# A gated linear recurrence on one core: its two directions run side by side instead of one after the other

## The chip, the cores and the metric

The kernel runs on one core of one Trainium2 chip. Its time is the device time of one execution in microseconds (us). Three executions of the kernel before took 5386.82, 5388.15 and 5391.06 us; the median is 5388.15. The engines of the core work side by side and wait for each other by semaphores: TensorE (PE in the profile; PEld is its loading of weights), VectorE (DVE), ScalarE (ACT), GpSimd (POOL) and SyncE (SP, which here only issues DMAs).

## The reference, cut to what matters

The program is a whole model: two hybrid layers (convolution, attention, Fourier mixing and a gated recurrence) and a second block. The change touches the recurrence alone, which each of the two hybrid layers holds once, in two directions over the positions:

```python
S_t = diag(f_t) S_{t-1} + k_t v_t^T          # per head, 64 x 64, four heads
o_t = S_t^T q_t
# in chunks, a = cumsum(log f) inside the chunk:
inter  = (q * exp(a)) @ state                # what earlier chunks give
scores[t, s] = sum_k q[t,k] k[s,k] exp(a[t,k] - a[s,k])   for s <= t
intra  = scores @ v
s_new  = exp(a_last) * state + (k * exp(a_last - a))^T @ v
```

Direction 0 goes from the first position to the last, direction 1 from the last to the first; both results are added. There are 10 tiles of 128 positions, two of them context. Layer 0 wants outputs for all 10; layer 1 wants them for 8 and runs the two context tiles only for the state. The kernel takes a chunk to be 128 positions.

## The kernel before

`recurrence` works on one direction. `mixer_layer` calls it twice, one block of the program after the other, with a barrier of all engines between them. Inside, one step of the loop is one tile of 128 positions (variable `u`). The scores of a tile can't be one product, since exp(a[t] - a[s]) may not be split into two factors at will. They are split into seven **levels**, `LEVELS = [64, 32, 16, 8, 4, 2, 1]`: at the level of half-width h the queries in one half of each 2h-wide group meet the keys in the other half, both scaled by exponentials relative to the boundary between the halves. An eighth product (`NL`) gives the diagonal. For each level:

- POOL subtracts the boundary value from the sums `a` (two instructions of 128x128 for each level, 14 for a tile) into `X`. There are two `X` buffers, taken in turn by tile.
- ACT exponentiates a whole `X` (one instruction of 1792 columns), and also gives `eq` and `ke`.
- DVE multiplies both halves by queries and keys (`scale_level`, two instructions for each level, 14 for a tile; `scale` for `ke` and `qe`).
- PE multiplies: four heads, each 128x128 with a contraction over 64 rows. The profile shows each float32 matmul as two records, so that two levels (one group g, of which a tile has four) are 16 records. A group goes to one of two pairs of PSUM banks, taken in turn.
- DVE copies all 128 columns of all four heads from PSUM to `sc`, only where the level's mask is set (`copy_predicated`, L1175, eight for a tile). Each such copy waits for the one before it, since all write `sc`.

When all eight copies are done PE makes the outputs of the tile (L1263 and L1264, 16 records), DVE copies them to `o` (L1197) or adds them (L1199, direction 1), and only then copies the first group of the next tile. Beside this, PE turns `ke` (L1219), ACT copies it from PSUM to `ket` (L1112), PE makes the state products (L1253), and DVE updates the state `S` (L1187).

In layer 0, PE also makes one piece of the modulation matrix for each tile (`Modulations.products`, L2565 and L2568, 72 records): its weights are a 2 MB chunk loaded by SP into a ring of three slots, and ACT evacuates it.

The order on each engine is the order in which the code is written; no scheduler moves anything.

Of the kernel before, what the change touches and what calls it, by code (L numbers as in the profile page):

```python
# [12 lines left out]
P = 128  # L13
# [1010 lines left out]
def recurrence(k, direction, q, key, a, v, o, outputs, lay, mods=None, moves=()):  # L1024

# [4 lines left out]
    X = [lay(f"x{i}", [P, NL, 2, P]) for i in range(2)]  # L1033
    eq = [lay(f"eq{i}", [P, 2, P]) for i in range(2)]
    qe = [lay(f"qe{i}", [P, 2, P]) for i in range(2)]
    ke = lay("ke", [P, 2, P])
    ket = lay("ket", [P, BR])
    sc = lay("sc", [P, 2, 2, P])
    masks = lay("masks", [P, NL + 1, P])
    S = [lay(f"s{i}", [P, 2, HD]) for i in range(2)]  # L1040
    order = [0, 1] + list(range(CT_, NT)) if direction == 0 else [1, 0] + list(range(NT - 1, CT_ - 1, -1))
    edge = P - 1 if direction == 0 else 0
    query_half = 1 if direction == 0 else 0
    want = [t in outputs for t in order]
    n_out = np.concatenate([[0], np.cumsum(want)]).astype(int).tolist()
    (masks_in, x_exped, subbed, exped, chain, scaled, products, masked, ke_t, ket_out, s_ready, state_out,
     o_ready, o_out, moved) = sems = k.sems(
        "masks_in", "x_exped", "subtracted", "exped", "dve_chain", "scaled", "level_products", "masked",
        "ke_transposed", "ket_out", "state_products", "state_out", "o_ready", "o_out", "moved")


    PAIRS = (NL + 1) // 2

    def halves(view, h):

        r = view.rearrange("p c (n s h) -> p c n s h", s=2, h=h)
        return [r[:, :, :, i, :] for i in range(2)]

    with nc.Block() as block:
        @block.sync  # L1060
        def _(sp):
            sp.dma_start(masks[:, :, :], d["level_masks"][direction]).then_inc(masks_in, 16)
            for dst, src in moves:
                sp.dma_start(dst, src).then_inc(moved, 16)
            k.ws.load_until(sp, k.ws.taken)
            if moves:
                sp.wait_ge(moved, 16 * len(moves))

        @block.gpsimd
        def _(pool):  # L1070
            for u, t in enumerate(order):
                if not want[u]:
                    continue
                j = n_out[u]
                at = a[:, :, t * P:(t + 1) * P]
                if j >= 2:
                    pool.wait_ge(products, PAIRS * (j - 1))
                for l, h in enumerate(LEVELS):
                    xa, xb = halves(X[j % 2][:, l, :, :], h)
                    aa, ab = halves(at, h)  # L1080
                    b = aa[:, :, :, h - 1:h] if direction == 0 else ab[:, :, :, 0:1]
                    b = b.to_broadcast([P, 2, P // (2 * h), h])
                    pool.tensor_tensor(xa, *((b, aa) if query_half else (aa, b)), ALU.subtract)
                    ins = pool.tensor_tensor(xb, *((ab, b) if query_half else (b, ab)), ALU.subtract)
                ins.then_inc(subbed, 1)

        @block.scalar
        def _(act):
            if mods:
                mods.load_bias(act, mods.first)  # L1090
                mods.load_bias(act, mods.first + 1)
            for u, t in enumerate(order):
                at = a[:, :, t * P:(t + 1) * P]
                if u >= 2:
                    act.wait_ge(state_out, u - 1)
                act.activation(eq[u % 2][:, :, :], at, ACT.Exp)
                if u >= 1:
# [2260 lines left out]
```

## Time and profile before

| what | value |
|---|---|
| median of three runs | 5388.15 us |
| the profiled execution | 5394.52 us, span 5392.5 us |
| recurrence, layer 0, both directions | 917.9 to 1259.5 us of the span |
| recurrence, layer 1, both directions | 2214.9 to 2500.3 us |
| busy over the whole span | PE 81%, DVE 53%, ACT 34%, POOL 11% |

The page of the profile gives these shares as a mean over stages with different limits. The change lies in two stretches that together are 627 us long, some 12% of the span. How long one tile takes there, and what ends each wait, is read from two views. The windows give one row for each stretch: its bounds and length in us, then the busy us and number of instructions of PE, PEld, DVE, ACT and POOL, the clock granted to TensorE as a share of 2.4 GHz (so 0.50 is 1.2 GHz and 1.00 is 2.4 GHz), the DMA share and GB/s. The timeline gives one row for each instruction, or run of equal ones: start in us, length in us, engine, line, operation, output<-inputs, shapes, count, and in brackets the idle time of the engine before it and what ended it. Starts of neighbouring rows give the pitch, which is less than the length where instructions overlap in an engine's pipeline.

### The profile page before, as it was taken

Reading aid. Unit: us, or ns where it says so; the run is one execution under the profiler, and the core shown is the slowest. Engines: PE = TensorE matmul, PEld = TensorE weight load, DVE = VectorE, ACT = ScalarE, POOL = GpSimd, SP = SyncE. Lnnn points to the kernel's source line nnn. Section 1 sums busy time; section 2 is a strip of 40 time slices with the busy share of each in tenths; the row PEclk is TensorE's granted clock in tenths of the full one; section 3 lists DMA queues with packets and bytes.
Section 4 is the critical chain, followed back from the end, with each engine's and each line's share of the span. In section 5 each row is a group of like instructions: output and inputs, shape, how many; then the busy total and the mean of one; then the engine's idle time right before and its main releaser. Section 6 shows DMA issues by size and latency. Waiting matters only on the chain. (4 is left out here: it accounts for less than half of the span.)

```text
span 5392.5 us, 56133 instructions
## 1 busy us (share of the span) xinstructions
PE 4351.5 (81%) x21480; PEld 3266.6 (61%) x21480; DVE 2869.4 (53%) x4265; ACT 1822.4 (34%) x3173; POOL 616.7 (11%) x858
## 2 busy tenths in 40 slices
PE   5758887877875988666677999997764969899898
PEld 4644576766664566555554655556652657688777
DVE  3454347665545546666543454542556745566545
ACT  3322245222432226312431333333322444344333
POOL 0001000330000100231001211110004500011100
PEclk7867899767887999767888999998886979899999
DMA  4000012333400011101200000003000054211134
GB/s 149 24 16 0 20 41 84 136 130 114 136 24 19 0 37 40 55 5 48 99 16 16 8 4 4 4 1 122 19 1 2 1 184 160 55 47 47 55 129 144
DMA packets 173564, 296.36 MB, mean 55 GB/s; under 512 B 43434, under 2 KB 94634, under 8 KB 173300
## 3 DMA queue, kind: packets, MB, share of 16 engines
q1 hardware_dynamic: 172548, 292.56, 16.1%
q8 instruction: 173, 2.83, 0.2%
q0 software_dynamic: 608, 0.08, 0.1%
q14 instruction: 91, 0.75, 0.0%
q10 hardware_dynamic: 144, 0.15, 0.0%
HBM read 262.25 MB, written 30.51 MB: 54 GB/s over the span
## 5 line engine op out<-in xcount | busy, mean ns | idle before, releaser
L319 DVE TENSOR_TENSOR x_low<-buf_a,x_high 128x1280 fp32r<-128x1280 f32 (+4 forms) x336 | 336.8, 1002 | 603.8 <-ACT x_high L297 602.0
L344 PE MATMUL ps<-x_high,w_high 128*128 128x256 f32 (+1 forms) x1344 | 492.4, 366 | 91.8 <-DVE w_low L323 89.1
L957 ACT ACTIVATE pt<-ps 128x512 f32<-128x512 f32 (+1 forms) x488 | 289.7, 594 | 752.3 <-PE ps L900 750.8
L297 ACT CAST x_high<-buf_a 128x1280 fp32r<-128x1280 f32 (+4 forms) x336 | 292.9, 872 | 726.6 <-PE ps L346 596.2
L910 PE MATMUL ps<-pt,v 128*128 128x512 f32 (+1 forms) x976 | 508.3, 603 | 0.0
L345 PE MATMUL ps<-x_low,w_high 128*128 128x256 f32 (+1 forms) x1344 | 486.8, 362 | 0.0
L346 PE MATMUL ps<-x_high,w_low 128*128 128x256 f32 (+1 forms) x1344 | 483.8, 360 | 0.0
L981 DVE TENSOR_REDUCE mx<-ps 128x1 f32<-128x1280 f32 (+1 forms) x200 | 289.8, 1449 | 350.9 <-PE ps L867 349.4
L2955 PE MATMUL ps<-w_high,x_high 128*128 128x512 f32 x896 | 369.6, 413 | 105.5 <-DVE w_low L2828 60.4
L2956 PE MATMUL ps<-w_low,x_high 128*128 128x512 f32 x896 | 362.8, 405 | 0.0
L2957 PE MATMUL ps<-w_high,x_low 128*128 128x512 f32 x896 | 362.7, 405 | 0.0
L344 PEld LDWEIGHTS ps<-x_high,w_high 128*128 128x128 f32 x1344 | 260.7, 194 | 153.7 <-DVE x_low L319 107.6
L2828 DVE TENSOR_TENSOR w_low<-w,w_high 128x1024 fp32r<-128x1024 f32 x170 | 208.2, 1225 | 255.6 <-ACT w_high L2925 255.6
L344 PE MATMUL ps<-w_high,x_high 128*128 128x512 f32 (+2 forms) x608 | 217.5, 358 | 110.6 <-DVE w_low L323 107.0
L898 PE MATMUL ps<-q_high,k_high 97*128 97x512 f32 (+3 forms) x488 | 292.1, 599 | 11.1 <-DVE q_low L994 11.1
L1003 DVE RECIPROCAL rec<-ps 64x512 f32<-64x512 f32 (+1 forms) x52 | 168.0, 3231 | 249.6 <-PE ps L910 249.6
L2925 ACT CAST w_high<-w 128x1024 fp32r<-128x1024 f32 x170 | 178.2, 1048 | 337.8 <-PE ps L2957 337.7
L2259 PE MATMUL ps<-x_high,w_high 128*128 128x512 f32 x704 | 278.2, 395 | 12.4 <-DVE w_low L2355 12.4
L346 PEld LDWEIGHTS ps<-x_high,w_low 128*128 128x128 f32 x1344 | 259.5, 193 | 39.0
L345 PEld LDWEIGHTS ps<-x_low,w_high 128*128 128x128 f32 x1344 | 260.7, 194 | 33.8
L2261 PE MATMUL ps<-x_high,w_low 128*128 128x512 f32 x704 | 279.6, 397 | 0.0
L2260 PE MATMUL ps<-x_low,w_high 128*128 128x512 f32 x704 | 278.9, 396 | 0.0
(388 smaller groups left out, 8757.9 us busy)
## 6 DMA issues: line engine op xcount, KB each, us to landing
w<-in_w_out SPq DMA_DIRECT2D x26, 2048.0 KB, 8.0
w<-in_w_mod SPq DMA_DIRECT2D x24, 2048.0 KB, 8.1
w<-in_w_down SPq DMA_DIRECT2D x15, 2048.0 KB, 7.9
w<-in_w_in SPq DMA_DIRECT2D x14, 2048.0 KB, 8.5
w<-in_w_up SPq DMA_DIRECT2D x22, 1024.0 KB, 7.6
w<-in_w_in SPq DMA_DIRECT2D x12, 1024.0 KB, 5.1
x<-in_x SPq DMA_DIRECT2D x16, 512.0 KB, 3.9
scratch_x<-x SPq DMA_DIRECT2D x16, 512.0 KB, 5.2
```

Source lines behind the costliest of these rows:

```text
L297: act.copy(xh[i % NX][:, 0:s["tn"]], x_of(s)).then_inc(x_high, 1)
L319: dve.tensor_tensor(xl[i % NX][:, 0:s["tn"]], x_of(s), xh[i % NX][:, 0:s["tn"]].bitcast(F32), ALU.subtract).then_inc(x_low, 1)
L344: pe.matmul(g["out"], lhs[0][:, :], rhs[0][:, :], start=(s["kk"] == 0), stop=False)
L345: pe.matmul(g["out"], lhs[0][:, :], rhs[1][:, :], start=False, stop=False)
L346: mm = pe.matmul(g["out"], lhs[1][:, :], rhs[0][:, :], start=False, stop=s["last"])
L898: pe.matmul(o, hi, qh[u % 2][r0:r1, 0:nq], start=True, stop=False)
L910: pe.matmul(ps[:, 6 + u % 2, 0:w["nq"]], w["v"](i), pt[g % NPT][:, 0:w["nq"]], start=(i == 0), stop=(i == n - 1)).then_inc(pv_done, 1)
L957: act.activation(pt[g % NPT][:, 0:w["nq"]], ps[:, 4 + g % 2, 0:w["nq"]], ACT.Exp, scale=scale).then_inc(exped, 1)
L981: dve.tensor_reduce(mx[u % 2][:, i:i + 1], src, AX.X, ALU.max).then_inc(maxed, 1)
L2955: pe.matmul(o, a[:, t], wh[i % NW][:, c], start=(s["kk"] == 0), stop=False)
L2956: pe.matmul(o, a[:, t], wl[i % NW][:, c], start=False, stop=False)
L2957: mm = pe.matmul(o, b[:, t], wh[i % NW][:, c], start=False, stop=s["last"])
```

## The change

One call of `recurrence` now runs both directions. A class `Scan` holds a direction's buffers, semaphores and its order of tiles, and the list `D2` holds the two. Every engine goes through the tile step by group, and inside a group does direction 0 and then direction 1:

- Each direction has one `x` buffer (not two), its own pair of PSUM banks for the level products (banks 0 and 1, or 2 and 3; a group has to be copied out before the next of that direction is made), and its own bank for keys and state (4 or 5). The output banks 6 and 7 are shared by the two in turn.
- POOL, ACT and the scaling on DVE work group by group for the next tile, each as soon as the group of this tile has been multiplied.
- A level's copy covers only the columns that are queries at that level (64 of 128 in each head, read and written with gaps for the small levels). The diagonal's copy stays whole.
- The outputs of tile u-1 are made at the start of tile u.
- The modulation pieces go two for each step of both directions, in free columns of banks 4 and 5, behind groups 2 and 3.
- The reload of `YT[:, 0:4]` from memory (2.5 MB), which ran beside direction 0, is now issued in `recurrence_norm`, whose SP waits for it at its end.
- `o` is written by whichever direction comes to a tile first, and the other adds.

The core of the diff (`r` is a `Scan`, G is 4):

```diff
+            for g in range(G):
+                for r in D2:
+                    subtract(r, first, g)
+            for u in range(first, NU - 1):
+                for g in range(G):
+                    for r in D2:
+                        pool.wait_ge(r.products, G * n_out[u] + g + 1)
+                        subtract(r, u + 1, g)
...
-                        dve.copy_predicated(
-                            sc[:, :, :, :].rearrange("p a b c -> p (a b) c"),
-                            masks[:, l, :].bitcast(U32).unsqueeze(1).to_broadcast([P, 4, P]),
...
+                    if l < NL:
+                        h = LEVELS[l]
+                        to, heads = (x.rearrange("p g (n s h) -> p g n s h", s=2, h=h)[:, :, :, r.query_half, :]
+                                     for x in (to, heads))
...
+                for g in range(G):
+                    for r in D2:
+                        if g == 0 and n_out[u]:
+                            output(r, u - 1)
+                        copies(r, u, g)
+                        if g == 0:
+                            scale_levels(r, u, G - 1)
+                        elif u + 1 < NU:
+                            scale_levels(r, u + 1, g - 1)
+                        if g == 1:
+                            state(r, u)
+                        if g == 2 and u + 1 < NU:
+                            scale(r, u + 1)
...
+            def level_products(r, u, g):
+                j = n_out[u]
+                pe.wait_ge(r.x_scaled, G * j + g + 1)
+                if j or g:
+                    pe.wait_ge(r.masked, (NL + 1) * j + 2 * g)
...
+                for g in range(G):
+                    for r in D2:
+                        if g == 0 and n_out[u]:
+                            outputs_of(r, u - 1)
+                        level_products(r, u, g)
+                        if g == 0:
+                            turn_keys(r, u)
+                        if g == 1:
+                            states(r, u)
+                    if mods and g >= 2:
+                        pe.wait_ge(D2[g - 2].state_out, u + 1)
+                        mods.products(pe, mods.first + 2 * u + g - 2)
...
-    for direction in range(2):
-        lay = Layout(k, A_A, A_B)
...
+    recurrence(k, q, key, a, v, o, range(nt0, NT), Layout(k, A_A, A_B), mods)
+    recurrence_norm(k, layer, o, YT, nt0, Layout(k, A_A, A_B), [(YT[:, 0:4, :], done_rows)])
```

How this moves instructions on VectorE, in the middle of a tile of layer 0. Before: `sc` is the score buffer, `x_152` one of the two operand buffers; a copy (L1175) stands between the two multiplications (L1154) of each level, and after the last of them the state (L1187) and the output.

```order
L1154 TENSOR_TENSOR x_152_6739<-x_152_6739,q_5132 128x4x32
L1175 COPY_PREDICATED sc_6747<-masks_6748,ps 128x512
L1154 TENSOR_TENSOR x_152_6739<-x_152_6739,key_125_5130 128x8x16
L1154 TENSOR_TENSOR x_152_6739<-x_152_6739,q_5132 128x8x16
L1175 COPY_PREDICATED sc_6747<-masks_6748,ps 128x512
L1154 TENSOR_TENSOR x_152_6739<-x_152_6739,key_125_5130 128x16x8
L1154 TENSOR_TENSOR x_152_6739<-x_152_6739,q_5132 128x16x8
L1175 COPY_PREDICATED sc_6747<-masks_6748,ps 128x512
L1154 TENSOR_TENSOR x_152_6739<-x_152_6739,key_125_5130 128x32x4
L1154 TENSOR_TENSOR x_152_6739<-x_152_6739,q_5132 128x32x4
L1175 COPY_PREDICATED sc_6747<-masks_6748,ps 128x512
L1154 TENSOR_TENSOR x_152_6739<-x_152_6739,key_125_5130 128x64x2
```
After: `sc_159` and `x_152` belong to direction 0, `sc_171` and `x_164` to direction 1; the shapes of the copies (L1159) show the gaps.

```order
L1159 COPY_PREDICATED sc_159_6746<-masks_160_6747,ps 128x16x16
L1159 COPY_PREDICATED sc_159_6746<-masks_160_6747,ps 128x32x8
L1138 TENSOR_TENSOR x_152_6739<-x_152_6739,key_125_5130 128x2x64
L1138 TENSOR_TENSOR x_152_6739<-x_152_6739,q_5132 128x2x64
L1138 TENSOR_TENSOR x_152_6739<-x_152_6739,key_125_5130 128x4x32
L1138 TENSOR_TENSOR x_152_6739<-x_152_6739,q_5132 128x4x32
L1164 SCALAR_TENSOR_TENSOR s_161_6748<-s_162_6749,eq_154_6741,ps 128x64 x2
L1159 COPY_PREDICATED sc_171_6757<-masks_172_6758,ps 128x16x16
L1159 COPY_PREDICATED sc_171_6757<-masks_172_6758,ps 128x32x8
L1138 TENSOR_TENSOR x_164_6750<-x_164_6750,q_5132 128x2x64
L1138 TENSOR_TENSOR x_164_6750<-x_164_6750,key_126_5131 128x2x64
L1138 TENSOR_TENSOR x_164_6750<-x_164_6750,q_5132 128x4x32
```
The copies now come in pairs of one direction, of 256 columns instead of 512, and the multiplications of that direction for the next tile (L1138) follow each pair.

How it moves them on TensorE, around the start of a tile. Before: the first group of a tile (`x_153`, L1243 x8), the keys' turn (L1219), two groups at once, the modulation piece (L2565, L2568), the last group, the state products (L1253) and the outputs (L1263, L1264) of the same tile.

```order
L1243 MATMUL ps<-x_153_6740 128x128 x8
L1219 MATMUL ps<-ident_49,ke_6745 128x128 x2
L1243 MATMUL ps<-x_153_6740 128x128 x16
L2565 MATMUL ps<-w_2_50,act_c_55 2x128 x32
L2568 MATMUL ps<-bias_148_6736,one_56 2x128 x4
L1243 MATMUL ps<-x_153_6740 128x128 x4
L1243 MATMUL ps<-q_5132,key_125_5130 128x128 x4
L1253 MATMUL ps<-v_5133,ket_6746 64x64 x4
L1263 MATMUL ps<-v_5133,sc_6747 128x64
L1264 MATMUL ps<-s_163_6750,qe_157_6744 128x64
L1263 MATMUL ps<-v_5133,sc_6747 128x64
L1264 MATMUL ps<-s_163_6750,qe_157_6744 128x64
```
After: the outputs of direction 1 for the tile before (`sc_171`, L1263 and L1264), then one group (L1249 x8) of each direction in turn, with the keys' turn (L1223) and the state products (L1231) between them.

```order
L1264 MATMUL ps<-s_173_6759,qe_167_6753 128x64
L1263 MATMUL ps<-v_5133,sc_171_6757 128x64
L1264 MATMUL ps<-s_173_6759,qe_167_6753 128x64
L1249 MATMUL ps<-x_164_6750 128x128 x8
L1223 MATMUL ps<-ident_49,ke_169_6755 128x128 x2
L1249 MATMUL ps<-x_152_6739 128x128 x8
L1231 MATMUL ps<-v_5133,ket_158_6745 64x64 x4
L1249 MATMUL ps<-x_164_6750 128x128 x8
L1231 MATMUL ps<-v_5133,ket_170_6756 64x64 x4
L1249 MATMUL ps<-x_152_6739 128x128 x8
L1249 MATMUL ps<-x_164_6750 128x128 x8
L2586 MATMUL ps<-w_3_51,act_c_55 2x128 x32
```
The outputs have gone from the end of their tile to the first group of the next, and no two groups of one direction stand next to each other.

## Rows read from the trace of the kernel before

**Rows 1.** Windows: the four direction blocks; busy us of each engine, TensorE clock, DMA.

```profile
917.00:1089.00 172.00, 136.94 (x1620) 115.01 (x1620) 106.95 (x272) 40.50 (x92) 56.09 (x141) 0.71 0.44 154
1089.00:1259.00 170.00, 136.75 (x1620) 114.63 (x1620) 107.33 (x272) 39.08 (x90) 56.37 (x140) 0.70 0.37 128
2214.00:2359.50 145.50, 95.70 (x740) 80.48 (x740) 88.76 (x224) 26.78 (x49) 43.84 (x112) 0.69 0.10 37
2359.50:2500.00 140.50, 95.82 (x740) 80.41 (x740) 87.24 (x224) 25.48 (x48) 44.32 (x112) 0.68 0.02 5
```
**Rows 2.** Timeline of VectorE, one tile (start, us, ..., idle before).

```profile
949.41 1.56 DVE L1175 COPY_PREDICATED sc<-masks,ps 128x512 f32<-128x512 uint32 x2 [1.49 <-PE ps L1243]
...
953.03 0.28 DVE L1154 TENSOR_TENSOR x<-x,q 128x128 f32<-128x128 f32 x1
953.23 0.75 DVE L1175 COPY_PREDICATED sc<-masks,ps 128x512 f32<-128x512 uint32 x1
953.87 0.28 DVE L1154 TENSOR_TENSOR x<-x,key 128x128 f32<-128x128 f32 x1
...
957.47 0.49 DVE L1154 TENSOR_TENSOR x<-x,q 128x128 f32<-128x128 f32 x1
957.88 0.72 DVE L1175 COPY_PREDICATED sc<-masks,ps 128x512 f32<-128x512 uint32 x1
...
959.99 0.46 DVE L1187 SCALAR_TENSOR_TENSOR s<-s,eq,ps 128x64 f32<-128x64 f32 x2
963.77 0.42 DVE L1197 COPY o<-ps 128x256 f32<-128x256 f32 x1 [3.32 <-PE ps L1264]
965.68 0.73 DVE L1175 COPY_PREDICATED sc<-masks,ps 128x512 f32<-128x512 uint32 x1 [1.49 <-PE ps L1243]
```
**Rows 3.** Timeline of TensorE, the same tile and the outputs before it.

```profile
943.18 0.43 PE L1263 MATMUL ps<-v,sc 128*128 128x64 f32 x2 [1.72 <-DVE sc L1175]
943.54 0.43 PE L1264 MATMUL ps<-s,qe 64*128 64x64 f32 x2
...
949.21 0.69 PE L1219 MATMUL ps<-ident,ke 128*128 128x128 f32 x2
949.82 2.60 PE L1243 MATMUL ps<-x 64*128 64x128 f32 x32
952.35 1.93 PE L2565 MATMUL ps<-w,act_c 128*2 128x128 f32 x64
...
955.63 0.45 PE L1253 MATMUL ps<-v,ket 128*64 128x64 f32 x8
958.75 0.66 PE L1263 MATMUL ps<-v,sc 128*128 128x64 f32 x2 [2.67 <-DVE sc L1175]
959.34 0.69 PE L1264 MATMUL ps<-s,qe 64*128 64x64 f32 x2
...
963.42 2.12 PE L1243 MATMUL ps<-x 64*128 64x128 f32 x15
```
**Rows 4.** Windows: TensorE's granted clock in three short stretches.

```profile
951.00:953.00 2.00, 2.00 (x50) 1.86 (x50) 1.60 (x4) 1.79 (x2) 0.00 (x0) 1.00 0.00 0
959.00:961.00 2.00, 2.00 (x8) 1.65 (x8) 1.45 (x5) 0.00 (x0) 2.00 (x6) 0.50 1.05 404
2640.00:2660.00 20.00, 10.55 (x48) 8.25 (x46) 13.17 (x23) 9.42 (x21) 0.00 (x0) 0.91 0.33 105
```
**Rows 5.** Timeline of VectorE: first copies of both layers, one scaling.

```profile
933.82 1.57 DVE L1175 COPY_PREDICATED sc<-masks,ps 128x512 f32<-128x512 uint32 x2 [2.18 <-PE ps L1243]
...
2234.75 0.28 DVE L1154 TENSOR_TENSOR x<-x,q 128x128 f32<-128x128 f32 x1
...
2237.28 1.58 DVE L1175 COPY_PREDICATED sc<-masks,ps 128x512 f32<-128x512 uint32 x2 [1.87 <-PE ps L1243]
```
**Rows 6.** DMA issues, start of layer 0's first block: KB each, us to landing.

```profile
buf_b<-scratch_branches SPq DMA_DIRECT2D x1, 2560.0 KB, 13.8
```
**Rows 7.** Timeline of SyncE: first DMA of the stage after `recurrence_norm`, layer 0.

```profile
1280.29 0.81 SPq L2970 DMA_DIRECT2D gate_row<-scratch_mod  x2
```

More of the change, by code:

```diff
@@ L1021, with recurrence @@
 NL = len(LEVELS)
-def recurrence(k, direction, q, key, a, v, o, outputs, lay, mods=None, moves=()):
+def recurrence(k, q, key, a, v, o, outputs, lay, mods=None):
     nc, ps, d = k.nc, k.ps, k.d
[L1033 to L1044, printed above, removed]
-    n_out = np.concatenate([[0], np.cumsum(want)]).astype(int).tolist()
[L1046 to L1057, printed above, removed]
+    D2 = [Scan(k, i, q, key[i], a[i], outputs, lay) for i in range(2)]
+    NU = NT
+    want = [t in outputs for t in D2[0].order]
+    n_out = np.concatenate([[0], np.cumsum(want)]).astype(int).tolist()
+    first = want.index(True)
+    G = (NL + 1) // 2
+    levels_of = lambda g: [l for l in (2 * g, 2 * g + 1) if l < NL]
+    writer = {}
+    for u in range(NU):
+        for r in D2:
+            if want[u]:
+                writer.setdefault(r.order[u], (r, n_out[u] + 1))
     with nc.Block() as block:
@@ L1202, in _, with scale @@
[L1202 to L1206 removed]
+            def scale(r, u):
+                dve.wait_ge(r.exped, u + 1)
+                dve.tensor_tensor(r.ke[:, :, :], r.ke[:, :, :], r.tile(r.key, u), ALU.mult).then_inc(r.ke_scaled, 1)
+                if want[u]:
+                    dve.tensor_tensor(r.qe[n_out[u] % 2][:, :, :], r.eq[u % 2][:, :, :], r.tile(r.q, u),
+                                      ALU.mult).then_inc(r.qe_scaled, 1)
@@ new lines, in turn_keys, with states @@
+            def turn_keys(r, u):
+                pe.wait_ge(r.ke_scaled, u + 1)
+                if u >= 1:
+                    pe.wait_ge(r.state_out, u)
+                    if mods:
+                        pe.wait_ge(mods.evacuated, 2 * (u - 1) + r.direction + 1)
+                for c in range(2):
+                    mm = pe.transpose(ps[:, r.keys_bank, c * P:(c + 1) * P], r.ke[:, c, :], k.ident[:, :])
+                mm.then_inc(r.ke_t, 1)
+            def states(r, u):
+                pe.wait_ge(r.ket_out, u + 1)
+                t = r.order[u]
@@ L1266, in recurrence @@
-    k.done(sems + (mods.sems if mods else []))
-def recurrence_norm(k, layer, o, yt, t_from, lay):
+                mm.then_inc(r.s_ready, 1)
+            def level_products(r, u, g):
+                j = n_out[u]
+                pe.wait_ge(r.x_scaled, G * j + g + 1)
+                if j or g:
+                    pe.wait_ge(r.masked, (NL + 1) * j + 2 * g)
+                for half in range(2):
+                    l = 2 * g + half
+                    for h in range(4):
+                        c, par = divmod(h, 2)
+                        p0 = par * HD
+                        x = y = r.x[p0:p0 + HD, min(l, NL - 1), c, :]
+                        if l == NL:
+                            x, y = r.tile(r.key, u)[p0:p0 + HD, c, :], r.tile(r.q, u)[p0:p0 + HD, c, :]
+                        o0 = c * 256 + half * P
+                        mm = pe.matmul(ps[:, r.bank + par, o0:o0 + P], x, y, start=True, stop=True)
+                mm.then_inc(r.products, 1)
@@ L1271, in recurrence_norm @@
+            for r in D2:
+                outputs_of(r, NU - 1)
+    k.done(D2[0].sems + D2[1].sems + (mods.sems if mods else []))
+def recurrence_norm(k, layer, o, yt, t_from, lay, moves):
     nc, ps, d = k.nc, k.ps, k.d
```

351 lines of the change are left out of this document (173 added, 178 removed).

## The prediction

> **What bounds the kernel now.** I looked first at the busy shares of the page, which name no single bound, and then at the windows over the two stretches that the change touches. The four direction blocks are 172, 170, 145.5 and 140.5 us long [rows 1], 628 us together, about 627 without the barriers at the edges. In none is an engine full: in a layer 0 block VectorE is busy 107 of 172 us, POOL 56, ACT 40. TensorE shows 137, but at a mean clock of 0.71, so much of that is work at half speed. What bounds a block is a chain, and the timeline of VectorE shows it. A tile is one lap: the first copy at 949.41, the same copy of the next tile at 965.68, so 16.3 us. VectorE is occupied from 949.4 to 960.5, then stands 3.32 us until the outputs are made, copies them for 0.42 us and stands again for 1.49 us until the first level group of the next tile is there [rows 2]. TensorE meanwhile stands 2.67 us before those outputs, and when it starts they run at a pitch of 0.59 to 0.62 us for two records, against 0.36 us in the tile before (943.18 to 943.54), and the first group after them takes 2.12 us for 15 records, against 2.60 us for 32 in the middle of the tile [rows 3]. The granted clock is 0.50 in the first place and 1.00 in the second [rows 4]. So each engine waits for the other once a tile, and TensorE's wait also costs it half its clock in the part that VectorE waits for.
>
> Steady laps give 15.5 us on average in layer 0: from the first copy at 933.8 to the end of that block at 1088 are 154 us for ten tiles, the start being 16 us [rows 1, 5]. In layer 1 the first copy is at 2237.3, 22.4 us after the start, and eight tiles take the remaining 122 us, 15.3 us each. A pair of tiles, one of each direction, costs 31.0 and 30.6 us. Below, P0 and P1 are what such a pair costs after the change.
>
> **VectorE's work for a pair.** The whole copy lasts 0.73 to 0.75 us, the next instruction starts 0.64 us after it (953.23 to 953.87), and two linked by their wait take 1.56 us, so a link costs about 0.8 us in all [rows 2]. Nothing here copies half the columns. The nearest rows are the instructions without a mask: 128 columns last 0.28, 256 last 0.42 us [rows 2], 0.14 us for each 128. Off 0.73 that makes 0.45 us for 256 columns, which I take; the other end is 0.73, if gaps cost as much as they save. A linked pair of half copies is then 0.45 + 0.08 + 0.37 = 0.9 us, and the last group, with the whole diagonal, 0.45 + 0.08 + 0.64 = 1.17. For each direction: three pairs 2.7, last 1.17, 14 multiplications at 0.20 (953.03 to 953.23) 2.8, ke and qe 0.7, state 0.46 + 0.08, outputs 0.42, in sum 8.3 us. A pair takes 16.7 us, against about 22 now (11.1 a tile, without the waits).
>
> The gaps are the point where a rule speaks against the change. The last multiplication of a tile, whose operands in SBUF alternate element by element, lasts 0.28 us like the one of the widest level [rows 2, 5], so gaps in SBUF are free here; gaps read from PSUM no row shows. The Trainium skill ("SBUF — State Buffer", section "Door 1: The DMA port swizzle") says that SBUF has lines of 16 bytes and PSUM of 8, that an access to a new line pays a penalty, and that gaps in PSUM slow matmuls significantly. For SBUF the trace doesn't agree; for PSUM it is silent, and I keep the case below as a rival, with its price from rows.
>
> POOL's subtractions now lie beside VectorE's work, no longer mostly in its idle time. Where both run, a multiplication starts 0.41 instead of 0.20 us after the last (957.47 to 957.88) while a copy stays at 0.72 [rows 2]. POOL is busy 5.6 us a tile [rows 1], 11.2 us a pair, near half of the time, so half of 32 such instructions pay 0.21 us: 3.3 us; the ends are 0 and 6.7. VectorE's sum is 16.7 + 3.3 = 20.
>
> **TensorE's work for a pair.** At full clock: eight groups of 16 records at 0.08 us (2.60 us for 32) are 10.2 us; outputs 2 x 16 x 0.18 (0.36 for two) 5.8; keys' turn 2 x 0.3, half of the 0.61 between 949.21 and 949.82; state products 2 x 0.45; modulation, layer 0 only, 2 x 2.2 (1.93 and the bias rows behind it) 4.4 [rows 3]. Together 21.9 in layer 0, 17.5 in layer 1. At half clock: groups 2 x 8 x 1.1 = 17.5, outputs 9.9 (0.62 for two), the rest doubled, 39 and 30.4 us. I expect full clock nearly throughout: waits in the new order are under 1.5 us, and TensorE holds 0.91 in a stretch where it is busy 10.6 of 20 us [rows 4]; but 959.3 shows what one wait of 2.67 us does.
>
> **The laps.** Go through the four groups g, with both directions in each. At g = 0 TensorE has 2 x (2.9 + 1.28 + 0.3) = 9.0 us and VectorE 3.4; at g = 1 TensorE 3.5 and VectorE 4.5; at g = 2 they have 2.6 (4.8 with the modulation) and 4.9; at g = 3 2.6 (4.8) and 3.9. A group of a direction may follow only when its previous one is copied, and VectorE does that while TensorE makes the other direction's group. In layer 0 VectorE falls behind by about 1 us at g = 1 and g = 2 and catches up during g = 3 and the outputs; the lap is TensorE's 21.9 us. In layer 1 VectorE leads from g = 1 to g = 3: 9.0 + 4.5 + 4.9 + 3.9 = 22.3, less some 1.4 us by which the last copies run beside the next outputs, 20.9. To both I add 2.5 us, that part of POOL's 3.3 us that falls outside g = 0, and wake-ups. P0 = 24.5, P1 = 23.5.
>
> The wait between the two outputs (the shared banks 6 and 7: direction 1 must wait for direction 0's copy, 0.42 us) is hidden, since a group and a turn of keys, 1.6 us, stand between them on TensorE. POOL (11.2) and ACT (40.5 / 10, so 8 a pair and some 1.5 for three more starts of each exponential [rows 1]) have half of the lap free; each step of theirs is for the next tile. Two 2 MB weight chunks in 24.5 us replace one in 15.5; each has two laps of slack in a ring of three.
>
> **What is saved once.** A second block's start goes in each layer, and the start that stays has both directions in it: twice the subtractions, but no 2.5 MB reload beside the masks. I leave it as it is, 16 and 22 us [rows 1, 5]. The end costs what the last lap saves by having no next tile. The reload took 13.8 us to land [rows 6]; `recurrence_norm` lasts from 1259 to 1280 [rows 1, 7], so it stays hidden, as it would in layer 1, whose stage is some 3 us shorter. If that cover failed it would cost at most a few us.
>
> **The sum.** Layer 0: 16 + 10 x 24.5 = 261. Layer 1: 22 + 8 x 23.5 = 210. Together 471 for 627, a gain of 156 us. Off the profiled execution's own 5394.5 that is 5238.5; that execution lies 6.4 us over the median, so off the median 5388.15 it is **5232 us**. In the general form the two stretches take 38 + 10 P0 + 8 P1, and no gain is left at 10 P0 + 8 P1 = 589.
>
> **The rivals.**
> - *TensorE alone is the bound.* POOL's share hurts only where VectorE has slack. P0 = 22, P1 = 21: 426, gain 201, 5187 us. For it: half of VectorE's collisions fall at g = 0. Against it: every hand-over of a single bank pair costs a wake-up.
> - *Copies with gaps are no cheaper.* The half copy stays at 0.73, 14 x 0.28 = 3.9 us a pair. Layer 0 hides most of it: P0 = 26, P1 = 27.2, together 516, gain 111, 5277 us. By the rule of the Trainium skill on PSUM lines (same page and section) this, or more, would be the cost of the copies of the small levels.
> - *The clock keeps falling.* TensorE, fed in bursts of 1.3 us, is at half speed half of the time: P0 = (21.9 + 39) / 2 = 30.5, P1 26.5, together 555, gain 72, 5316 us. For it: 0.68 to 0.71 over the blocks now [rows 1]. Against it: its long waits are what goes.
> - *The slower side: half clock throughout.* The alternation leaves TensorE waiting at each group, so that it never gets its clock back; then P0 = 39 and P1 = 30.5, together 672, 45 us more, 5433 us. It decides when over about two thirds of TensorE's work in layer 0 is at 1.2 GHz. Against it: at half clock in layer 0 TensorE would have no wait at all, and a run without waits got its clock back here, by 951 [rows 4].
>
> **How the numbers follow.** My forecast has 52%, TensorE alone 15%, no cheaper copies 14%, the falling clock 14%, the slower side 3%, and 2% for no difference through something I haven't seen. About 0.2% (11 us) is what a measurement can tell from no change. The range, 5175 to 5325, takes in the three milder rivals with the ends of the half copy and of POOL's share, and leaves out the slower side. Faster 0.95, within 0.2% 0.02, slower 0.03.
>
> **What would show it.** In the profile after: one block for each layer, near 261 and 210 us; the same copy of one direction every 24 us; half copies at 0.45 us; TensorE's clock over 0.9 in the block, and outputs at 0.36 us for two records; VectorE's longest waits at g = 0, for the outputs' end. Half copies near 0.73, a block clock under 0.8, or multiplications at 0.41 nearly everywhere would prove a step wrong, and with P0 over 28 the forecast is.

## The result, and the profile after

The changed kernel takes 5267.52 us (median of 4 runs, 5256.10 to 5277.01); before, on the same chip, 5389.60 (5386.82 to 5398.37). The ratio is 0.9766 with a 95% interval of 0.9753 to 0.978, so 2.3% faster. The forecast was 5232 us with a range of 5175 to 5325: the side and the range hold, the median is 35.5 us over the forecast. The profiled execution took 5277.01 us.

The page after, busy time by engine over the whole span:

```profile
PE 4310.9 (82%) x21480; PEld 3235.0 (61%) x21480; DVE 2825.0 (54%) x4265; ACT 1845.9 (35%) x3281; POOL 612.5 (12%) x858
```

As before, that doesn't show the change. The windows do. Each hybrid layer now has one recurrence block, here from its first DMA (the masks) to the first DMA of `recurrence_norm` (columns as in [rows 1]); the last two rows are 25 us out of the middle of each:

```profile
918.12:1168.36 250.24, 216.05 (x3240) 180.71 (x3240) 189.70 (x544) 91.99 (x241) 109.75 (x280) 0.90 0.51 183
2128.93:2375.67 246.74, 197.43 (x1480) 166.37 (x1480) 156.87 (x448) 63.35 (x145) 86.74 (x224) 0.63 0.04 14
...
1015.00:1040.00 25.00, 22.04 (x373) 18.65 (x377) 21.56 (x63) 10.30 (x26) 13.09 (x34) 1.00 0.48 170
...
2260.00:2285.00 25.00, 20.74 (x159) 17.48 (x158) 18.58 (x53) 7.14 (x16) 10.74 (x28) 0.64 0.01 1
```

Cut in the same way, the blocks before were 341.6 and 285.4 us. The sum goes from 627.0 to 497.0, 130 us less (forecast 156). The profiled executions differ by 117.5 us (5394.52 and 5277.01); the other 12.6 us are in stages that the change doesn't touch, 0.2 ahead of the first block, 5.1 between the two and 7.3 behind the second. Among all the traces of this study the stretch between the blocks is 955.4 to 961.7 us long, and the one ahead of the first block 903.9 to 919.6, though its code is the same in all; I take both for variation from run to run, and what sets them was not looked into. A difference of some 15 us between two single executions can therefore come from outside the blocks. The blocks vary too: four traces in which the layer 0 block is the same code show 247.2 to 254.9 us for it, and layer 1's unchanged block 244.8 to 246.7. Differences of some 8 us in layer 0 mean nothing below.

The two rows in the middle are the finding: in the middle of layer 0 TensorE is at its full clock (0.90 over the whole block), in layer 1 it has a granted clock of 0.64, less than in the old blocks (0.68 to 0.71, [rows 1]).

Timeline of TensorE after, one lap of layer 0 (the copy of direction 0's first group starts at 1004.64, and again at 1028.42):

```profile
1001.04 0.43 PE L1264 MATMUL ps<-s,qe 64*128 64x64 f32 x2
1001.40 0.43 PE L1263 MATMUL ps<-v,sc 128*128 128x64 f32 x2
...
1013.42 1.16 PE L1249 MATMUL ps<-x 64*128 64x128 f32 x16
1015.74 1.16 PE L1249 MATMUL ps<-x 64*128 64x128 f32 x16 [1.16 <-DVE sc L1159]
1016.83 1.93 PE L2586 MATMUL ps<-w,act_c 128*2 128x128 f32 x64
1018.69 0.40 PE L2589 MATMUL ps<-bias,one 1*2 1x128 f32 x8
...
1021.18 0.72 PE L1249 MATMUL ps<-x 64*128 64x128 f32 x8 [1.00 <-DVE sc L1159]
```

Two waits of about 1 us are left, and the outputs stand at a pitch of 0.36 us; in [rows 3] there was one wait of 2.67 us and outputs at 0.59. The same in layer 1:

```profile
2276.32 0.72 PE L1249 MATMUL ps<-x 64*128 64x128 f32 x8 [2.10 <-DVE sc L1159]
2276.84 0.64 PE L1249 MATMUL ps<-q,key 64*128 64x128 f32 x8
2278.98 1.23 PE L1249 MATMUL ps<-x 64*128 64x128 f32 x8 [1.50 <-DVE sc L1159]
2279.97 1.09 PE L1249 MATMUL ps<-q,key 64*128 64x128 f32 x8
2281.67 0.69 PE L1263 MATMUL ps<-v,sc 128*128 128x64 f32 x2 [0.61 <-DVE sc L1159]
2282.29 0.69 PE L1264 MATMUL ps<-s,qe 64*128 64x64 f32 x2
...
2286.37 2.12 PE L1249 MATMUL ps<-x 64*128 64x128 f32 x15
```

Three waits follow one another (2.10, 1.50, 0.61). The group at 2278.98 is already twice as long as the one at 2276.32, and outputs and first group run at half speed, at 0.62 and 2.12 us as in [rows 3]. The old fault is back in this layer.

Timeline of VectorE after: in layer 0 a pair of copies of the groups g = 1, 2 and 3; then, in layer 1, the lap's start, its longest wait and its end:

```profile
1014.69 0.90 DVE L1159 COPY_PREDICATED sc<-masks,ps 128x256 f32<-128x256 uint32 x2
...
1017.26 1.23 DVE L1159 COPY_PREDICATED sc<-masks,ps 128x256 f32<-128x256 uint32 x2
...
1024.59 1.48 DVE L1159 COPY_PREDICATED sc<-masks,ps 128x256 f32<-128x256 uint32 x2
```

```profile
2259.71 0.92 DVE L1159 COPY_PREDICATED sc<-masks,ps 128x256 f32<-128x256 uint32 x2 [1.39 <-PE ps L1249]
...
2264.96 0.42 DVE L1177 COPY o<-ps 128x256 f32<-128x256 f32 x1 [3.53 <-PE ps L1264]
...
2288.52 0.92 DVE L1159 COPY_PREDICATED sc<-masks,ps 128x256 f32<-128x256 uint32 x2 [1.39 <-PE ps L1249]
```

A pair of half copies takes 0.90 us as forecast for half-widths 64 to 8. The pair of 4 and 2 takes 1.2, that of 1 and the diagonal 1.5: single copies last 0.42 to 0.44 us down to half-width 4, and 0.73 to 0.75 at 2 and 1, as long as a whole one [rows 2]. The layer 1 lap is 2288.52 - 2259.71 = 28.81 us.

### The profile page after: what moved, and what is told of

It reads as the page before. It is cut to its first block and busy times, and to the rows that moved or that the text cites. A ratio compares the mean times of both kernels' runs of the same rounds, so it can differ in the third digit from the quotient of the medians.

```text
span 5275.2 us, 56171 instructions
## 1 busy us (share of the span) xinstructions
PE 4310.9 (82%) x21480; PEld 3235.0 (61%) x21480; DVE 2825.0 (54%) x4265; ACT 1845.9 (35%) x3281; POOL 612.5 (12%) x858
## 3 DMA queue, kind: packets, MB, share of 16 engines
q1 hardware_dynamic: 172548, 292.56, 16.3%
```

## The experiments

My theory after the result: in layer 1, which has no modulation work, TensorE's waits cost it its clock, and the half clock costs the missing 5 us a lap. The rivals: VectorE's dearer small copies, or POOL's share of its time. Each run is given as a ratio to the kernel before, timed on the same chip (medians there 5395.47, 5393.97 and 5397.81 us for the three sets), and with its two blocks (layer 0 / layer 1), cut as above; the changed kernel has 250.2 / 246.7.

**filled.** Unneeded matmuls behind groups 2 and 3 of layer 1, into a free part of a bank, all on the same two rows.

```diff
+            def fill(n):
+                for i in range(n):
+                    pe.matmul(ps[0:2, 6, 256:384], k.ident[:, 0:2], k.ident[:, :], start=True, stop=True,
+                              skip_group_check=True)
...
+                        if not mods:
+                            fill({(2, 0): 16, (2, 1): 24, (3, 0): 20, (3, 1): 8}.get((g, r.direction), 0))
```

> The changed kernel, with unneeded small matmuls (2 output rows, never read) in layer 1 alone, where TensorE waits for the copies: 16 behind direction 0's group 2, 24 behind direction 1's, 20 and 8 behind the two of group 3; at the 0.029 us a record seen for the modulation matmuls that is some 4 us of added TensorE work for each pair of tiles. Theory (the clock in layer 1 falls because TensorE waits 1.5 to 2.1 us at groups 2 and 3, and the outputs that follow then run at half speed): the granted clock in layer 1 rises from 0.64 to over 0.9, a pair of tiles falls from 28.8 to 22.5 to 24 us, the block from 247 to about 205, the time by about 40 us against the changed kernel. Rival (VectorE or the hand-over of the banks sets the lap in layer 1): the lap stays at 28 to 29 us or grows by the added work, up to 33 us.

Measured: 5291.44 us, 0.9804 [0.9787, 0.982], blocks 250.3 / 272.0: slower than without, where the theory had 40 us less. The timeline of TensorE says why:

```profile
2251.96 3.65 PE L1269 MATMUL ps<-ident 128*2 128x128 f32 x32
2255.55 1.16 PE L1249 MATMUL ps<-x 64*128 64x128 f32 x16
2256.64 5.40 PE L1269 MATMUL ps<-ident 128*2 128x128 f32 x48
...
2270.45 0.43 PE L1263 MATMUL ps<-v,sc 128*128 128x64 f32 x2
2270.81 0.43 PE L1264 MATMUL ps<-s,qe 64*128 64x64 f32 x2
...
2273.21 1.16 PE L1249 MATMUL ps<-x 64*128 64x128 f32 x15
```

The clock is back (outputs at 0.36, first group 1.16, granted clock 0.95 over the block), but a record of the filling took 0.114 us (3.65 / 32) where the modulation's takes 0.030 (1.93 / 64), so the filling itself became the bound. The modulation's matmuls go to four groups of rows in turn; these wrote the same rows every time.

**filled4.** The same numbers of matmuls, spread over four groups of rows.

```diff
+                    q = 32 * (i % 4)
+                    pe.matmul(ps[q:q + 2, 6, 256:384], k.ident[:, 0:2], k.ident[:, :], start=True, stop=True,
```

> As the run filled, but the unneeded matmuls of layer 1 write to four groups of output rows in turn (as the modulation matmuls do, 0.029 us a record), where those of the run filled all wrote to the same two rows and took 0.115 us a record. So 0.93, 1.4, 1.2 and 0.5 us of added TensorE work at the four places, not 3.7, 5.4, 4.5 and 1.9. Theory (the clock in layer 1 falls through TensorE's waits, and full clock is worth 5 us a lap): clock in the block over 0.9, lap 22.5 to 24.5, block 200 to 215 us, 30 to 45 us under the changed kernel. Rival (what the clock gives back, the added matmuls and VectorE's chain take): lap 27 to 29, the same time within 8 us.

Measured: 5251.14 us (5245.18 to 5254.91), 0.973 [0.9712, 0.9748], blocks 254.9 / 236.0. It is the fastest version that leaves nothing out: all its runs are under all of **after_again**, the changed kernel once more on the same chip.

> The changed kernel itself, beside the others on the same chip: 5260 to 5275 us, laps of 23.8 and 28.8 us, as a base for the differences.

That gave 5268.70 us (5257.05 to 5277.63), 0.9762 [0.974, 0.9784], blocks 247.2 / 246.6. Its median is 17.6 us over that of filled4. The two profiled executions differ by 13.1 us, of which layer 1 gives 10.6, the unchanged stretch ahead of the first block another 10.6, and layer 0 takes 7.7 back. The gain falls short of the 30 to 45 us of the theory, and the expected lap of 22.5 to 24.5 us was missed; it is 27.2 (the filling's records now take 0.031 to 0.033 us). The timeline of TensorE in filled4:

```profile
2203.00 1.49 PE L1270 MATMUL ps<-ident 128*2 128x128 f32 x48
...
2207.23 0.71 PE L1249 MATMUL ps<-x 64*128 64x128 f32 x8 [0.45 <-DVE sc L1159]
...
2209.93 0.43 PE L1263 MATMUL ps<-v,sc 128*128 128x64 f32 x2 [0.99 <-DVE sc L1159]
...
2212.11 0.46 PE L1263 MATMUL ps<-v,sc 128*128 128x64 f32 x2
...
2212.89 2.12 PE L1249 MATMUL ps<-x 64*128 64x128 f32 x15
```

Two short waits stay, and the clock falls in the middle of the outputs; the first group is at half clock again. The block's clock is 0.74. So the clock is worth at least the 10.6 us by which this block is shorter than in after_again. The slow filling of `filled`, which left no wait at all, held the clock; a quick one that leaves none was not tried. Why layer 1 loses its clock at waits (0.45 and 0.99) that layer 0 stands (1.16 and 1.00) is open.

**fewer_products.** Layer 0 with less work for TensorE: one of eight row blocks of each modulation piece.

```diff
-        for kk in range(KD):
+        for kk in range(KD if self.first == 0 else 1):
```

> The changed kernel with one of the eight row blocks of the modulation products left out of all that are made beside the recurrence of layer 0 but the first (8 of the 64 records of a piece stay, with the bias), so about 1.6 us less TensorE work for each piece, 3.2 us for a pair of tiles. Theory (layer 0 has its full clock only because the modulation pieces fill TensorE's waits): layer 0's clock falls from 0.93 to 1.00 to about 0.65, its lap grows from 23.8 to 27 to 29 us though it has less to do, and the time grows by 30 to 50 us. Rival (TensorE's work sets the lap, the clock is independent of it): the lap falls by up to 3 us, to 21 us, and the time by up to 30 us.

Measured: 5307.43 us, 0.9838 [0.9824, 0.9853], blocks 298.1 / 244.8. TensorE has 3.1 us less to do in each lap, two pieces of 1.93 us shrunk to 0.40, and layer 0 is 48 us slower (the median of the whole kernel 40 us, 30 to 50 were expected): its clock fell from 0.90 to 0.62. In the timeline of TensorE the pattern of layer 1 appears in layer 0:

```profile
1047.72 1.23 PE L1249 MATMUL ps<-x 64*128 64x128 f32 x8 [1.04 <-DVE sc L1159]
...
1053.38 0.69 PE L1263 MATMUL ps<-v,sc 128*128 128x64 f32 x2
1053.99 0.69 PE L1264 MATMUL ps<-s,qe 64*128 64x64 f32 x2
```

This is the strongest evidence for the theory: nothing but TensorE's own work was changed, and downward.

**full_copies.** Only the copies are widened again to all 128 columns.

```diff
-                    if l < NL:
+                    if l < 0:
```

> The changed kernel with all copies over all 512 columns again: this undoes the copies over query columns alone. By the durations in the trace after (0.44 us for half-widths 64 to 4, 0.73 for 2 and 1, whole 0.74) each pair of tiles gets 2 x 5 x 0.30 = 3.0 us more on VectorE. Theory (VectorE leads only in groups 1 to 3): layer 0's lap grows by 1 to 2.5 us, layer 1's by 2 to 3 us, together 25 to 50 us more than the changed kernel. Rival (the narrow copies gave nothing, the order of the work gave all): the same time within 10 us.

Measured: 5295.23 us, 0.9816 [0.9798, 0.9834], blocks 277.2 / 251.1. The narrow copies are worth 27 us in layer 0, part of it by the clock (0.82 instead of 0.90), and 4 in layer 1, where VectorE has waits of 3.5 us to fill. The median is 28 us over that of the changed kernel, inside the 25 to 50 expected, but layer 1's lap grew by 0.6 us and not by 2 to 3.

**less_pool.** Three of seven levels of POOL's subtractions for later tiles are gone (POOL is busy 69 instead of 110 us in layer 0). The exponentials are taken of zero times the input, so the scores are not the reference's.

```diff
-                for l in levels_of(g):
+                for l in levels_of(g) if u == first else levels_of(g)[-1:]:
...
-                act.activation(x, x, ACT.Exp).then_inc(r.x_exped, 1)
+                act.activation(x, x, ACT.Exp, scale=0.0).then_inc(r.x_exped, 1)
```

> The changed kernel with POOL doing only the last level's two subtractions of each group for all tiles but the first, and the level exponentials taken of zero times the input (so the scores are not the reference's, the instructions of all other engines and their shapes are the same). POOL's instructions for a pair of tiles fall from 28 to 16. Theory (POOL costs VectorE about 0.2 us for each multiplication that meets it, worth 2.5 us of the lap in my sum): layer 0's lap falls by 1 to 1.5 us and layer 1's by as much, 15 to 25 us in all. Rival (these collisions fall where VectorE waits for TensorE anyway): laps within 0.5 us, under 10 us in all.

Measured: 5247.94 us, 0.9724 [0.971, 0.9739], blocks 246.5 / 236.5. The median is 19.6 us under that of the changed kernel, inside the 15 to 25 expected, and 14 us of it are in the blocks of the traces; the laps of layer 0 gained 0.4 us where 1 to 1.5 were expected, those of layer 1 gained 1.3. A multiplication lasts 0.30 us on average, not 0.36. So POOL's share of VectorE's time is worth 10 us in layer 1, and in layer 0 no more than that block varies, for three sevenths of its instructions: real, but not the missing 37, and the clock in layer 1 stayed at 0.63.

**before_narrow.** The other way round: the old order, with the narrow copies alone.

```diff
+                        if l < NL:
+                            h = LEVELS[l]
+                            to, heads = (x.rearrange("p g (n s h) -> p g n s h", s=2, h=h)[:, :, :, query_half, :]
+                                         for x in (to, heads))
```

> The kernel before with one part of the change alone: copies over query columns only, for all seven levels (the level products lie in PSUM as in the changed kernel so that four heads' halves can be read). By the durations in the trace after, five of the eight copies of a tile get 0.30 us shorter, 1.5 us for each tile. Theory (the lap of one direction is a chain through VectorE, so nearly all of it counts): 36 tiles by 1.0 to 1.5 us, 36 to 54 us off, so 5335 to 5355. Rival (TensorE waits less for the outputs but makes them at the same half clock, and its own groups become the bound): 5 to 30 us off.

Measured: 5377.31 us (10 runs), 0.9967 [0.9955, 0.9978], blocks 335.6 / 269.6. Only 17 us (of 5393.97; by the two blocks of the traces 22); the theory's 36 to 54 are missed. Timeline of VectorE there:

```profile
950.61 0.42 DVE L1136 TENSOR_TENSOR ke<-ke,key 128x256 f32<-128x256 f32 x1 [0.83 <-ACT ke L1100]
...
952.20 0.29 DVE L1154 TENSOR_TENSOR x<-x,key 128x128 f32<-128x128 f32 x1 [0.48 <-ACT x L1106]
...
962.32 0.42 DVE L1203 COPY o<-ps 128x256 f32<-128x256 f32 x1 [3.35 <-PE ps L1270]
```

Much of the time taken off the copies turned up as waits for ACT. In the same tile of the kernel before they are only 0.26 us for `ke` and 0.17 for `x`; over all tiles they grew from 17.0 to 35.6 us and from 6.5 to 18.4. The wait for the outputs at half clock stayed as it was (3.32 before).

**whole_small.** In the changed kernel the copies at half-widths 2 and 1 are whole again.

```diff
-                    if l < NL:
+                    if l < 5:
```

> The changed kernel with the two copies of half-widths 2 and 1 whole again, the other five narrow. In the trace after, these last 0.73 to 0.75 us for 256 columns, as much as 0.74 for 512. Theory (runs of one or two 4-byte elements cost twice, so narrowing them saves nothing): the same time as the changed kernel within 6 us, copies of 0.73. Rival (the whole copies are slower where POOL or TensorE also reads, or the pair's link differs): 10 us more.

Measured: 5264.66 us (5258.28 to 5271.19), 0.9761 [0.9743, 0.9779], blocks 249.7 / 244.6: the same as the changed kernel. Narrowing these two gains nothing.

**dense_a and dense_b.** Which operand's gaps cost? For half-width 2, a makes the PSUM source dense and b the mask; for 1, a makes destination and mask dense and b the destination alone. A dense operand takes the first 64 columns of each head, so wrong columns are copied.

```diff
+                        dense = {2: ('heads',), 1: ('to', 'which')}.get(h, ())      # dense_a
+                        dense = {2: ('which',), 1: ('to',)}.get(h, ())              # dense_b
```

> The changed kernel, with the operands' gaps taken away in part (wrong columns, so the scores are not the reference's): for half-width 2 the PSUM source is read densely and destination and mask keep their gaps; for half-width 1 destination and mask are dense and the PSUM source keeps its gaps. If the gaps in PSUM are what costs, half-width 2 falls from 0.73 to 0.44 us and half-width 1 stays at 0.74; if it is the gaps in SBUF (destination or mask), half-width 2 stays and half-width 1 falls to 0.44.

> As the run dense_a, with other operands: for half-width 2 the mask alone is dense, for half-width 1 the destination alone. If the mask's gaps cost, half-width 2 falls to 0.44 us; if the destination's, half-width 1 falls; if the PSUM source's, both stay at 0.73.

Measured: 5260.80 and 5267.22 us in a single run each, blocks 247.8 / 242.5 and 247.8 / 242.7. Timeline of VectorE in dense_a, the pair of half-widths 4 and 2, and then the pair of 1 and the diagonal:

```profile
2269.73 1.18 DVE L1162 COPY_PREDICATED sc<-masks,ps 128x256 f32<-128x256 uint32 x2
...
2272.59 1.19 DVE L1162 COPY_PREDICATED sc<-masks,ps 128x256 f32<-128x256 uint32 x2
```

The same two pairs in dense_b:

```profile
2273.01 1.17 DVE L1162 COPY_PREDICATED sc<-masks,ps 128x256 f32<-128x256 uint32 x2
...
2275.87 1.19 DVE L1162 COPY_PREDICATED sc<-masks,ps 128x256 f32<-128x256 uint32 x2
```

With source or mask dense, the pair of 4 and 2 stays at 1.2. With the destination dense, the pair of 1 and the diagonal falls from 1.5 to 1.19, in both kernels, with the PSUM source still read at every second element. The destination's gaps cost; those of source and mask are free in these copies. The copy at half-width 4, in runs of four float32, pays nothing; runs of two and of one pay the same.

**before_filled and before_filled_narrow.** How much of the gain is the clock alone? The old order, with 44 unneeded matmuls (28 in the second) for each wanted tile, ahead of the outputs.

```diff
+                    for i in range(44):
+                        r0 = 32 * (i % 4)
+                        pe.matmul(ps[r0:r0 + 2, 6, 256:384], k.ident[:, 0:2], k.ident[:, :], start=True, stop=True,
+                                  skip_group_check=True)
```

> The kernel before, with 44 unneeded small matmuls (four groups of output rows in turn, never read) between the state products and the outputs of each wanted tile, about 2.5 us of TensorE work in a wait of 2.7 to 3.0 us. Nothing else of the change is in it. Theory (half clock is what makes the outputs and the next first group slow, so the interleaving gains in part by keeping the clock): outputs at 0.36 instead of 0.62 us for two records, first group 1.2 instead of 2.1 us, some 3 us for each of 36 tiles, 70 to 110 us off. Rival (the clock isn't tied to this wait, or the added work delays the outputs): within 15 us of the kernel before.

> The run before_filled with the narrow copies as well and 28 matmuls (1.6 us) for the shorter wait: both gains that need no second direction. Theory (clock and copies are two separate gains, and side by side adds the overlap of the two chains to them): 15 to 50 us under before_filled, and still above the changed kernel with its clock kept, since each tile keeps VectorE's wait of 2.5 to 3 us for outputs and first group. Rival (all that the change gave is clock and copies): as fast as the changed kernel or faster, 5220 to 5265.

Measured: 5327.98 us (5325.86 to 5328.95), 0.9873 [0.9853, 0.9893], blocks 302.9 / 251.8, and 5290.71 us (5289.38 to 5316.34), 0.9816 [0.9788, 0.9843], blocks 293.3 / 247.1. Timeline of TensorE in before_filled, one tile of layer 0:

```profile
968.55 2.58 PE L1261 MATMUL ps<-ident 128*2 128x128 f32 x88
971.24 0.44 PE L1267 MATMUL ps<-v,sc 128*128 128x64 f32 x2
971.60 0.43 PE L1268 MATMUL ps<-s,qe 64*128 64x64 f32 x2
...
974.00 1.16 PE L1243 MATMUL ps<-x 64*128 64x128 f32 x15
```

The wait of 2.67 us is filled; outputs at 0.36, first group at 1.16. Useless work in an idle stretch takes 70 us off a kernel in which nothing else is changed, the lower edge of what was expected; the granted clock of the blocks is 0.88 and 0.85 (0.70 and 0.68 before). On top of it the narrow copies bring 37 us by the medians, twice the 17 they bring without it. The profiled execution of before_filled_narrow is the slowest of its four (5316.34 us), and its blocks are only 14 us shorter than those of before_filled. Its tiles in layer 0 show what held it back. Two windows, each from the start of one filling to the start of the next:

```profile
954.15:969.44 15.29, 14.68 (x223) 12.41 (x219) 9.72 (x30) 3.88 (x9) 5.65 (x15) 0.78 0.40 140
969.44:981.11 11.67, 11.57 (x223) 9.66 (x219) 8.65 (x27) 3.88 (x9) 5.50 (x15) 1.00 0.50 183
```

Timeline of TensorE, the start of the outputs in the first of them:

```profile
956.48 0.43 PE L1273 MATMUL ps<-v,sc 128*128 128x64 f32 x2 [0.61 <-DVE sc L1185]
```

The first seven such stretches of the block alternate. In one the outputs follow the filling at once, the clock stays full, and it takes 11.7 us. In the other a wait of 0.61 us is left behind the filling, the clock falls in the middle of the outputs, and it takes 15.3. Two of the short kind, 23.3 us, are as short as the changed kernel's average lap in layer 0 (23.4, below). Each short one but the first follows a long one, in which ACT and POOL may get ahead, so a steady 11.7 is not shown; a filling that leaves no wait beside the narrow copies was not tried.

## Why the prediction was right, and where its sum was wrong

**The bound, read from [rows 2 to 4]: shown.** The prediction took the old block for a chain in which one wait of TensorE also costs half its clock. On one chip the steps are: before 5397.8, with the clock mostly held 5328.0, with narrow copies too 5290.7, side by side 5268.7. So 70 of the 129 us are to be had by the clock alone, 37 by the narrow copies once the clock is held better, and 22 are left. Each step is a difference of medians; for the last the intervals of the ratios (0.9788 to 0.9843, and 0.974 to 0.9784) just don't touch, and by the blocks of the profiled executions the last two steps are 14 and 47. How these 59 us divide is therefore uncertain, and that the last step is due to the new order as such is not shown: in the profiled execution the old order lost its clock in every second tile of a long row, and was as fast as the new one in the others. The order is not needed to hold the clock: filling the wait raised it to 0.88 and 0.85. In layer 0 it holds most of it without useless work (0.90), in layer 1 it doesn't (0.63).

**What is saved once: right.** The first copies start 16.3 us (934.46) and 21.4 us (2150.35) after the block, forecast 16 and 22. `recurrence_norm` with the reload takes 20.8 us in layer 0 as before, so the reload is hidden:

```profile
1168.36 0.37 SPq L1305 DMA_DIRECT2D gain<-in_hgrn_norm_g  x1
1168.78 0.46 SPq L1307 DMA_DIRECT2D buf_b<-scratch_branches  x1
1189.20 0.82 SPq L2991 DMA_DIRECT2D gate_row<-scratch_mod  x2
```

**P0 = 24.5: a little high, and close in part by luck.** Ten laps take 1168.36 - 934.46 = 233.9 us, 23.4 each. In the lap from 1004.64 to 1028.42 TensorE works 23.78 - 2.16 = 21.6 us, forecast 21.9, but two errors cancel there: a group of 16 records has a pitch of 1.09 us at full clock and not 1.3 (the 2.60 us for 32 records in [rows 3] began at half clock), and this lap runs some 1.6 us longer because its first groups are at half clock. In a lap all at full clock TensorE works 20.07 us and waits 2.2. Laps of 22.3 and 23.8 us occur; the windows are such a short lap whole, then a stretch of a lap of 23.8 us, and one of the short lap:

```profile
1028.42:1050.71 22.29, 20.07 (x325) 16.81 (x326) 18.91 (x54) 9.10 (x24) 10.87 (x28) 1.00 0.54 189
1007.40:1011.90 4.50, 4.50 (x44) 3.80 (x44) 2.33 (x6) 1.50 (x4) 1.70 (x5) 0.62 0.14 52
1053.50:1058.00 4.50, 4.50 (x70) 3.84 (x70) 3.62 (x10) 1.97 (x6) 3.22 (x9) 1.00 0.19 70
```

The last window lies in the lap that starts at 1050.71. Layer 0 came out at 250 us, 11 better than forecast.

**P1 = 23.5: the step that failed.** Eight laps take 2375.67 - 2150.35 = 225.3 us, 28.2 each, and layer 1 came out 37 us over its 210. The sentence that failed is "I expect full clock nearly throughout: waits in the new order are under 1.5 us". For the laps I had worked out that VectorE leads from g = 1 to g = 3 in layer 1, which is to say that TensorE waits three times in a row there (2.10, 1.50, 0.61, the first beyond my 1.5), and I priced only the waits, not what follows them. It also rested on a row of another stage, where TensorE holds 0.91 though half idle [rows 4]; this stage shows that such a row doesn't carry over. From the pitches in the lap, half clock costs outputs 2 x 8 x (0.62 - 0.36) = 4.2 us, the two groups beside them 2 x (2.12 - 1.16) = 1.9, and the following groups, the keys' turns and the last group some 3 more; about 9 us, of which waits that were there anyway swallow a part. The lap is 5.3 us over the forecast. The rival "the clock keeps falling" was right for layer 1 (26.5, even too low) and wrong for layer 0 (30.5), because I had given both layers one answer; its 26.5 also held 2.5 us that its P0 didn't, since the mean of 17.5 and 30.4 is 24. Shown are that loss of the clock slows the lap (fewer_products) and that holding more of it shortens layer 1 (filled4, 10.6 us of the 37); that it explains all 37 is argued from the pitches only.

The Trainium skill ("TensorE: Matmul & The Clock Gate", section "A second HAM failure mode: psum-queue depth-cycling") describes a kernel whose short idle times between groups of matmuls let the clock go back and forth between its two levels. The rows of layer 1 agree: full speed at 2276.32, half at 2278.98.

**VectorE's work: the sum right, two terms off.** In the layer 1 lap its waits are 3.53 + 0.92 + 1.95 and twice 1.39, 9.2 us, so it works 19.6; forecast 20. The half copy at 0.45 us holds for five of seven levels; the last two cost 0.73, 4 x 0.29 = 1.2 us more a lap. Against that POOL took some 2.2 us (28 multiplications at 0.36 instead of 0.28), not 3.3. The rival of dearer copies had the wrong extent, and whole_small shows that narrowing those two changes nothing. The prediction looked for the cost in the gaps of the PSUM source and called gaps in SBUF free, by a row of a multiplication; dense_b shows that for this copy it is the other way round.

Of the prediction's tests, the block length of layer 0, outputs at 0.36 and VectorE's longest waits at g = 0 came out; "a block clock under 0.8" was named as what would prove a step wrong, and it did so for layer 1. The sum: -11 in layer 0, +37 in layer 1, +12.6 in untouched stages give the 38.5 us by which the profiled execution is over its forecast (5277.0 for 5238.5). One division in it was off without weight: 154 us for ten tiles are 15.4 each, not 15.5.

## What to carry to other kernels

Where TensorE waits once or more in each lap, price what follows the wait at half clock, lap by lap and stage by stage; a stage with other work between the waits tells nothing about one without it. Before an order is rebuilt to shorten such a chain, fill the wait with unneeded matmuls for one run: it tells at once how much the clock costs at least. Then look whether a wait is left: in before_filled_narrow 0.61 us of waiting was followed by half clock in every second tile. And where two engines take turns, time taken off one of them pays only if nothing else is late next: the narrow copies were worth 17 us, some 14 to 37, or 27 in one layer, depending on what stood around them.

## What the runs showed of the hardware

- Taking work away from TensorE (3.1 us a lap) made layer 0 48 us slower, through the granted clock (0.90 to 0.62).
- In the first seven tiles of before_filled_narrow, those in which TensorE had no wait ahead of the outputs show a granted clock of 1.00 and take 11.7 us; those with a wait of 0.61 us there show 0.78 and take 15.3.
- Matmuls with two output rows and 128 columns cost 0.031 to 0.033 us a record when they go to four groups of rows in turn, and 0.114 when each writes the rows of the one before.
- COPY_PREDICATED from PSUM to SBUF with 256 columns: 0.43 us with a destination in runs of four float32 or more, 0.73 in runs of two or one, whatever the gaps of the PSUM source and the mask. The Trainium skill ("SBUF — State Buffer", section "Door 1: The DMA port swizzle") gives SBUF lines of 16 bytes, four float32, and a penalty for each new one; the destination agrees: 64 such lines are touched at half-width 4, 128 at 2, at 1 and in a whole copy of 512 columns, and the last three all take 0.73 to 0.75 us. What it says of gaps in PSUM, for matmuls, no run here shows for them; for this copy they were free. A multiplication with the same gaps in SBUF is not slowed (0.28 us).
